# Moving three pieces of the SwiGLU "up" stage: an ACT split, a halved reciprocal and a divided last product

## The chip, the cores and the metric

One core of a Trainium2 chip runs the whole program. The metric is device time in microseconds (us) of one execution, from the host's request to the end on the core. TensorE is called PE (its weight loads PEld), VectorE DVE, ScalarE ACT, GpSimd POOL and SyncE, which issues the loads, SP.

## The reference

The program is one inference step of a two-layer decoder over 512 prompt tokens and 8 sample tokens. Every layer is a mixer with a residual and then a SwiGLU feed-forward block with a residual; layer 0 mixes with a gated convolution and a chunk MLP, layer 1 with a sparse attention. The change sits in the first half of the feed-forward block, which both layers have:

```python
D_MODEL = 1024
D_FF = ((8 * D_MODEL + 2) // 3 + 255) // 256 * 256   # 2816

def rmsnorm(x, g):
    xf = x.astype(jnp.float32)
    y = xf * lax.rsqrt(jnp.mean(xf * xf, axis=-1, keepdims=True) + EPS)
    return (y * g.astype(jnp.float32)).astype(x.dtype)

def swiglu(x, w_in, w_out):
    a, b = jnp.split(x @ w_in, 2, axis=-1)
    return (jax.nn.silu(a) * b) @ w_out

    # in each layer, for prompt xp and sample xs
    xp = xp + swiglu(rmsnorm(xp, norm_ffn[layer]), w_ffn_in[layer], w_ffn_out[layer])
```

## The kernel before, in words

Activations lie transposed, features on the 128 partitions and the 520 tokens (two halves of 260) along the free dimension. Every fp32 operand of a matmul is split into a high and a low part, and each product is three matmuls: high by high, high weight by low activation, low weight by high activation. For weights ACT writes the high part (`act_high`, line 706, 128x512) and POOL the low part (`pool_low`, line 714, raw minus high).

The stage that the change touches is the input projection of SwiGLU, called "up0" and "up1". Its 2816 columns a and 2816 columns b form 22 pairs of 128 columns (KF = 22). Each pair is computed as a block product with **seven** products instead of eight (Winograd's form): `A11`, `S1`, `S2`, `A12`, `S3`, `A22`, `S4`. S1 to S4 are sums and differences of weight blocks that DVE makes (`dve_sum`), from blocks that ACT first copies into PSUM (`act_copy`, line 694). A product is 4 quarters of 3 matmuls, so 12 matmuls of 128x260. PE's order for pair p is written out in `PE_SEQ`: A11(p), A22(p-1), S4(p-1), S1(p), S2(p), A12(p), S3(p), and then A11(p+1). The results are put together by:

- the copy of the first product, `first(p)` (line 965): ACT copies product A11 out of PSUM to `X1`. For p > 0 it waits for the last reader of the previous X1, the addition at line 909;
- `u2` (line 897), `u3` (lines 901 and 904), `up_rows` (909 adds X1 to A22's result, 911 multiplies by RSTD into TB) and `gate_rows` (916, 918) on DVE, then Silu on ACT (971), the gate (925), and the split of the result into G high (977) and G low (931), the operand of the next stage, "down".

PE waits for weights by a count on POOL's low parts (`u_lo`), and in some places for DVE: S3 waits for u2, A22 for u3, S2 also for the multiplication at 911, because it writes the PSUM bank that 911 reads. A12 waits for the X1 copy (`u_first`).

RSTD is the reciprocal root of the mean square per token. ACT writes the root (line 592), and DVE takes the reciprocal of all 520 columns at once in `norm_dve` (line 596) and clears ACC (597). The two lines are shared with other norms of the program; for the up stages they run at p = 1, between DVE's sum S2(1) and `up_rows(0)`.

The first pair's products are interleaved with the end of the stage before: `act_out_blocks` and `dve_out_blocks` finish the last tiles (m = 6, 7) of the output projection, turn its result into the right-hand blocks of the block product (lines 767 to 786 on ACT, 817 to 836 on DVE) and already split the first pair's weights. In the first pair PE computes three quarters of S2 and of A12, then the sum of squares (`pe_stat`), then their last quarters, because the last right-hand quarter comes late.

Each engine works through its own queue in program order; the order across engines is set by semaphores alone. SP loads the raw weights of pair p+2 when POOL has made the low part of A22(p).

The functions that the diff touches, with what calls them:

Of the kernel before, what the change touches and what calls it, by code (L numbers as in the profile page):

```python
# [21 lines left out]
HALF = T // 2  # L22
# [4 lines left out]
KF = FF // P  # L27
# [16 lines left out]
S0, U0 = {}, {}  # L44
# [128 lines left out]
def program(nc, a, out):  # L173
    ctx = ExitStack()
    with ctx:
# [351 lines left out]
        def plain(act):  # L527

            act.sem_inc(passed, 1)
# [213 lines left out]
            u_sum.on(ins)  # L743


        def act_out_blocks(act, l):

            name, i, gcol = f"out{l}", 2 * l + 1, G_FFN[l]
            for m in range(KD):
                q, x = m // 2, XT[:, m, :]  # L750
                gain = GAINS[:, gcol + m:gcol + m + 1]
                if m in (0, 2, 4):
                    split_next_wide(act, name, m // 4, m % 4 // 2)
                if m == 6:
                    act.wait_ge(tile_done.sem, U0[name] + 6)
                    act_copy(act, l, 0, "A21")
                    act_copy(act, l, 0, "A22")
                    act_high(act, l, 0, "A11")
                    act_high(act, l, 0, "S1")
                    act_high(act, l, 0, "S3")  # L760
                    act_copy(act, l, 0, "A12")
                    act_high(act, l, 0, "S2")
                if m == 7:
                    act_high(act, l, 0, "A12")
                act.wait_ge(tile_out.sem, m + U0[name] + 3)
                plain(act)
                b_full.on(act.activation(TA[:, m % 2, :], x, ACT.Copy, scale=gain))  # L767

                def square():
                    act.wait_ge(acc_ok.sem, m + 9 * (i - 1))  # L770
                    plain(act)
                    a_sq.on(act.activation(TG[:, m % 2, :], x, ACT.Square))
                if m % 2 == 0:
                    plain(act)
                    b_high.on(act.activation(x_part("B11", 0, q), x[:, 0:HALF], ACT.Copy, scale=gain))
                    act.wait_ge(b_turn.sem, 12 * l + 3 * q + 1)
                    plain(act)
                    b_high.on(act.activation(x_part("T1", 0, q), TB[:, 0:HALF], ACT.Copy))
                    square()
                else:  # L780
                    square()
                    plain(act)
                    b_high.on(act.activation(FB[:, 0:2, q, :], halves(x), ACT.Copy, scale=gain))
                    act.wait_ge(b_turn.sem, 12 * l + 3 * q + 3)
                    plain(act)
                    b_high.on(act.activation(HB[:, 1:4, q, :], HBR[:, 5:8, q, :], ACT.Copy))
# [53 lines left out]
        def pe_up(pe, l):  # L840

            name = f"up{l}"

            def product(p, op, qs=range(4)):
                par, other = (U0[name] + p) % 2, OTHER[op]
                bank = M[:, 2, 0:HALF] if op in ("S2", "S3", "A22") else PG[:, par, int(op in ("S1", "S4")), 0:HALF]
                wh, wl = home(WH, l, op), home(WL, l, op)
                for q in qs:
                    if p == 0:
                        pe.wait_ge(b_ok.sem, 16 * l + 4 * q + {"B11": 1, "T1": 2, "B21": 3, "B22": 3}.get(other, 4))  # L850
                    for n, w in ((0, wh), (1, wh), (0, wl)):
                        mm = pe.matmul(bank, w[:, q * P:(q + 1) * P], x_part(other, n, q),  # L852
                                       start=op in ("A11", "S1", "S2") and q == 0 and n == 0 and w is wh,
                                       stop=op in ("A12", "A22", "S4") and q == 3 and w is wl,
                                       skip_group_check=True)
                if q == 3:
                    (tile_done if op in ("A12", "S4") else u_prod).on(mm)

            for p, op in PE_SEQ:
                pe.wait_ge(u_lo.sem, 7 * KF * l + LO_NO[p, op])  # L860
                if op == "A11":
                    if p < 2:
                        pe.wait_ge(tile_out.sem, U0[name] + 1 + p)
                    elif p - 2 < LATE:
                        pe.wait_ge(g_ready.sem, G0[f"down{l}"] + p - 1)
                    else:
                        pe.wait_ge(t_gate.sem, KF * l + p - 1)
                if op == "S2" and p:
                    pe.wait_ge(tile_out.sem, U0[name] + 2 * p + 1)
                if op == "A12":  # L870
                    pe.wait_ge(u_first.sem, KF * l + p + 1)
                if op in ("S3", "A22", "S4"):
                    pe.wait_ge(u_add.sem, 4 * KF * l + 4 * p + {"S3": 1, "A22": 2, "S4": 3}[op])
                if (p, op) == (0, "S2"):
                    product(p, op, range(3))
                elif (p, op) == (0, "A12"):
                    product(p, op, range(3))
                    pe.wait_ge(u_sum.sem, 4 * KF * l + SUM_NO[0, "S4"])
                    pe_stat(pe, 2 * l + 1)
                    product(0, "S2", [3])  # L880
                    product(0, "A12", [3])
                else:
                    product(p, op)

        def dve_up(dve, l):
# [13 lines left out]
            def u3(p):  # L899
                wait_product(dve, l, p, "S3")  # L900
                u_add.on(dve.tensor_tensor(U3, turn(p)[1], X1[:, :], ALU.add))
                dve.wait_ge(u_add.sem, u_add.now)
                wait_product(dve, l, p, "S1")
                u_add.on(dve.tensor_tensor(W, turn(p)[2], U3, ALU.add))

            def up_rows(p):
                Y = turn(p)[1]
                wait_product(dve, l, p, "A22")
                u_add.on(dve.tensor_tensor(Y, Y, X1[:, :], ALU.add))
                dve.wait_ge(u_add.sem, u_add.now)  # L910
                tile_out.on(dve.tensor_tensor(halves(TB[:, :]), M[:, 2:4, 0:HALF], halves(RSTD[:, :]), ALU.mult))

# [20 lines left out]
            for p in range(KF + 1):  # L933
                if p:
                    u3(p - 1)
                    if p < KF:
                        dve_sum(dve, l, p, "S2")
                    if p == 1:
                        norm_dve(dve, 2 * l + 1)
                    up_rows(p - 1)  # L940
                    gate_rows(p - 1)
                    if p < KF:
                        dve_sum(dve, l, p, "S4")
                    gate(p - 1)
                if p < KF:
                    u2(p)
                if p + 1 < KF:
                    dve_sum(dve, l, p + 1, "S1")
                if 0 < p <= LATE:
                    g_low(p - 1)  # L950
                if p + 1 < KF:
                    dve_sum(dve, l, p + 1, "S3")
            for p in range(LATE, KF):
                g_low(p)

        def act_up(act, l):

            name, down = f"up{l}", f"down{l}"

            def first(p):  # L960
                wait_product(act, l, p, "A11")
                if p:
                    act.wait_ge(u_add.sem, 4 * KF * l + 4 * p)
                plain(act)
                u_first.on(act.activation(X1[:, :], PG[:, (U0[name] + p) % 2, 0, 0:HALF], ACT.Copy))

            def silu(p):
                both = sets((U0[name] + p) % 2)
# [10 lines left out]
            for p in range(KF):  # L979
                nxt = p + 1 < KF  # L980
                if p:
                    act_high(act, l, p, "S3")
                    act_copy(act, l, p, "A12")
                first(p)
                if p:
                    act_high(act, l, p, "S2")
                act_high(act, l, p, "A22")
                if nxt:
                    act_high(act, l, p + 1, "A11")
                if p == 0:  # L990
                    norm_act(act, 2 * l + 1)
                if p:
                    silu(p - 1)
                if p == 0:
                    act.wait_ge(a_std.sem, 2 * l + 2)
                if nxt:
                    act_copy(act, l, p + 1, "A21")
                    act_copy(act, l, p + 1, "A22")
                if 0 < p <= LATE:
                    g_high(p - 1)  # L1000
                act_high(act, l, p, "S4")
                if nxt:
                    act_high(act, l, p + 1, "S1")
                    act_high(act, l, p + 1, "A12")
# [1539 lines left out]
```

## Time and profile before

| | |
|---|---|
| median of 3 runs | 1343.24 us (1341.97 to 1344.81) |
| the profiled execution | 1342.97 us, its span 1341.2 us |
| mean granted TensorE clock | 0.995 of full |
| PE busy | 96% of the span |
| POOL, DVE, ACT busy | 60%, 54%, 48% |

The span runs from the first to the last instruction; the 1.77 us between it and the execution's time lie outside. PE's busy time is an upper figure: a matmul's duration overlaps the next one's, so that rows of 0.28 us start 0.12 us apart. The stages up0 and up1 lie at about 194 to 429 us and 966 to 1201 us; the stages down0 and down1 follow each.

### The profile page before, as it was taken

The page shows a single profiled execution, that of the slowest core. Times are in us where ns is not written, and L with a number is a line of the kernel's source. Part 1 is how long each engine was busy: PE and PEld are TensorE (multiplying, and loading weights), DVE is VectorE, ACT ScalarE, POOL GpSimd, SP SyncE. Part 2 cuts the span into 40 slices and gives each one's busy share as a digit, 9 for nine tenths or more (in the row PEclk, how much of TensorE's full clock was granted, in tenths as well). Part 3 has the DMA queues.
Part 4 walks back from the last instruction along what each step waited for, and adds up shares of the span by engine and source line. Part 5 has one row for each costly group of instructions (what it writes and reads, how often), then busy time and mean ns, then how long its engine had stood idle before and what let it go on. Part 6 is the DMA issues. An engine that isn't in the chain of part 4 may idle for free. (4 is left out here: it accounts for less than half of the span.)

```text
span 1341.2 us, 27440 instructions
## 1 busy us (share of the span) xinstructions
PE 1284.5 (96%) x10530; PEld 1193.9 (89%) x10530; DVE 721.1 (54%) x1213; ACT 644.7 (48%) x1160; POOL 808.9 (60%) x703
## 2 busy tenths in 40 slices
PE   6999999999999999999998998989999999999997
PEld 6999998999999999999986555657989999999997
DVE  5448587776776222211755767654877767761112
ACT  5412466666665233311313566653666666652332
POOL 7435447888888666644311554442578888886662
PEclk9999999999999999999999999999999999999999
DMA  5322223334333233337864042031233343333331
GB/s 182 95 95 69 91 64 95 95 110 112 95 95 97 87 86 88 115 96 167 195 143 89 18 139 66 1 87 32 64 95 96 105 116 96 95 97 87 87 102 68
DMA packets 211067, 127.87 MB, mean 95 GB/s; under 512 B 31868, under 2 KB 206004, under 8 KB 210958
## 3 DMA queue, kind: packets, MB, share of 16 engines
q1 hardware_dynamic: 210958, 126.40, 34.1%
q8 instruction: 70, 1.15, 0.4%
q14 instruction: 39, 0.32, 0.1%
HBM read 117.82 MB, written 5.38 MB: 92 GB/s over the span
## 5 line engine op out<-in xcount | busy, mean ns | idle before, releaser
L2177 POOL TENSOR_TENSOR WL<-WR,WH 128x512 fp32r<-128x512 f32 x236 | 317.6, 1377 | 274.6 <-ACT WH L537 274.6
L477 PE MATMUL PG<-G,WH 128*128 128x260 f32 x1856 | 298.9, 283 | 3.5 <-POOL WL L2177 3.5
L477 PEld LDWEIGHTS PG<-G,WH 128*128 128x128 f32 x1856 | 253.2, 188 | 6.3 <-POOL WL L2177 5.8
L537 ACT ACTIVATE WH<-WR 128x2048 fp32r<-128x2048 f32 x59 | 112.9, 1914 | 284.8 <-PE PG L477 249.2
L477 PE MATMUL PG<-H,WH 128*128 128x260 f32 x1312 | 216.6, 287 | 4.3 <-DVE H L2398 2.3
L852 PE MATMUL M<-HB,WH 128*128 128x260 f32 x1056 | 202.9, 290 | 8.4 <-POOL WL L714 4.9
L477 PE MATMUL PG<-G,WL 128*128 128x260 f32 x928 | 186.8, 282 | 0.0
L477 PEld LDWEIGHTS PG<-H,WH 128*128 128x128 f32 x1312 | 180.5, 190 | 6.4 <-POOL WL L2177 2.3
L714 POOL TENSOR_TENSOR WL<-WR,WH 128x512 fp32r<-128x512 f32 x132 | 169.5, 1297 | 21.1 <-ACT WH L706 21.1
L852 PEld LDWEIGHTS M<-HB,WH 128*128 128x128 f32 x1056 | 164.1, 190 | 18.1 <-POOL WL L714 15.6
L1323 POOL TENSOR_SCALAR PB<-PB,ST,GT 128x512 f32<-128x512 f32 (+3 forms) x128 | 80.1, 635 | 130.9 <-DVE ST L1776 130.4
L852 PE MATMUL PG<-FB,WH 128*128 128x260 f32 x528 | 149.3, 283 | 1.6 <-issue 1.6
L852 PE MATMUL M<-HB,WL 128*128 128x260 f32 x528 | 149.8, 284 | 0.0
L852 PE MATMUL PG<-FB,WL 128*128 128x260 f32 x528 | 148.8, 282 | 0.0
L477 PEld LDWEIGHTS PG<-G,WL 128*128 128x128 f32 x928 | 142.7, 188 | 0.0
L477 PE MATMUL PG<-H,WL 128*128 128x260 f32 x656 | 132.8, 284 | 0.0
L714 POOL TENSOR_TENSOR WL<-WLR,WH 128x512 fp32r<-128x512 f32 x90 | 114.6, 1294 | 3.3 <-ACT WH L706 3.3
L616 DVE TENSOR_TENSOR XT<-XT,PG 128x520 f32 x16 | 11.1, 697 | 174.7 <-PE PG L477 174.7
L477 PEld LDWEIGHTS PG<-H,WL 128*128 128x128 f32 x656 | 101.6, 189 | 0.0
L852 PEld LDWEIGHTS PG<-FB,WH 128*128 128x128 f32 x528 | 99.6, 189 | 1.9 <-issue 1.9
L852 PEld LDWEIGHTS M<-HB,WL 128*128 128x128 f32 x528 | 100.7, 191 | 0.0
L714 POOL TENSOR_TENSOR WL<-S2T,WH 128x512 fp32r<-128x512 f32 x44 | 57.5, 1306 | 71.5 <-ACT WH L706 71.5
(289 smaller groups left out, 2451.6 us busy)
## 6 DMA issues: line engine op xcount, KB each, us to landing
WR<-in_w_ffn_in SPq DMA_DIRECT2D x88, 512.0 KB, 4.9
WR<-in_w_in SPq DMA_DIRECT2D x32, 512.0 KB, 4.6
WR<-in_w_ffn_out SPq DMA_DIRECT2D x32, 384.0 KB, 4.1
WR<-in_w_ffn_out SPq DMA_DIRECT2D x32, 320.0 KB, 3.4
WR<-in_w_in SPq DMA_DIRECT2D x18, 256.0 KB, 4.4
WR<-in_w_out SPq DMA_DIRECT2D x8, 512.0 KB, 4.0
PST<-in_cache_kv SPq DMA_DIRECT2D x32, 128.0 KB, 2.3
WR<-in_w_out SPq DMA_DIRECT2D x16, 256.0 KB, 5.1
```

The costliest lines, as they stand in the source:

```text
L477: mm = pe.matmul(PG[:, par, hf, 0:HALF], w, x, start=(first and at_k == 0 and n == 0), stop=(last and at_k == nk - 1 and n == 2))
L537: w_hi.on(act.activation(WH[:, b, :], WR[:, b, :], ACT.Copy))
L616: tile_out.on(dve.tensor_tensor(row(XT, m), row(XT, m), sets((U0[name] + c) % 2), ALU.add))
L714: u_lo.on(pool.tensor_tensor(four(home(WL, l, op)), src, four(home(WH, l, op)).bitcast(F32), ALU.subtract))
L852: mm = pe.matmul(bank, w[:, q * P:(q + 1) * P], x_part(other, n, q), start=op in ("A11", "S1", "S2") and q == 0 and n == 0 and w is wh, st ...
L1323: p_ready.on(pool.tensor_scalar(pj, pj, ST8[:, 24 + o:25 + o], GT[:, i, g:g + 1], ALU.mult, ALU.mult))
L2177: low = pool.tensor_tensor(WL[:, b, c:c + 512], WR[:, b, c:c + 512], WH[:, b, c:c + 512].bitcast(F32), ALU.subtract)
```

## The change

- **ACT, p > 0**: the high part of S2(p) is split ahead of the X1 copy of the same pair instead of behind it. The order of the high parts among themselves stays.
- **ACT, p = 0**: the first X1 copy moves into `act_out_blocks`, at m = 7 behind the squares, ahead of the last splits of the right-hand blocks (783 and 786). It was the first instruction of `act_up`.
- **DVE**: the reciprocal of RSTD is taken in two halves of 260 columns. The first stands behind u2(0), ahead of the sum S1(1); the second stands inside `up_rows(0)`, between the addition at 909 and the multiplication at 911. The clearing of ACC goes to the end of p = 2. The sum S3(1) moves from the end of p = 0 to behind u3(0).
- **PE, last pair (p = 21)**: A12 is done in two parts, quarters 0 and 1 ahead of S3 and quarters 2 and 3 behind it.

```diff
+        def act_first(act, l, p):
+
+            wait_product(act, l, p, "A11")
+            if p:
+                act.wait_ge(u_add.sem, 4 * KF * l + 4 * p)
+            plain(act)
+            u_first.on(act.activation(X1[:, :], PG[:, (U0[f"up{l}"] + p) % 2, 0, 0:HALF], ACT.Copy))
+
         def act_out_blocks(act, l):
...
                     square()
+                    if m == 7:
+                        act_first(act, l, 0)
                     plain(act)
                     b_high.on(act.activation(FB[:, 0:2, q, :], halves(x), ACT.Copy, scale=gain))
...
+                elif (p, op) == (KF - 1, "A12"):
+                    product(p, op, range(2))
+                elif (p, op) == (KF - 1, "S3"):
+                    product(p, op)
+                    product(p, "A12", range(2, 4))
                 else:
                     product(p, op)
...
+            def rstd(hf):
+
+                dve.wait_ge(a_std.sem, 2 * l + 2)
+                r = RSTD[:, hf * HALF:(hf + 1) * HALF]
+                (rstd_ok if hf else vec).on(dve.reciprocal(r, r))
+                if hf:
+                    dve.wait_ge(vec.sem, vec.now)
+                    dve.wait_ge(rstd_ok.sem, rstd_ok.now)
+
             def up_rows(p):
                 Y = turn(p)[1]
                 wait_product(dve, l, p, "A22")
                 u_add.on(dve.tensor_tensor(Y, Y, X1[:, :], ALU.add))
+                if p == 0:
+                    rstd(1)
                 dve.wait_ge(u_add.sem, u_add.now)
                 tile_out.on(dve.tensor_tensor(halves(TB[:, :]), M[:, 2:4, 0:HALF], halves(RSTD[:, :]), ALU.mult))
...
             for p in range(KF + 1):
                 if p:
                     u3(p - 1)
+                    if p == 1:
+                        dve_sum(dve, l, p, "S3")
                     if p < KF:
                         dve_sum(dve, l, p, "S2")
-                    if p == 1:
-                        norm_dve(dve, 2 * l + 1)
                     up_rows(p - 1)
                     gate_rows(p - 1)
                     if p < KF:
...
                 if p < KF:
                     u2(p)
+                if p == 0:
+                    rstd(0)
                 if p + 1 < KF:
                     dve_sum(dve, l, p + 1, "S1")
                 if 0 < p <= LATE:
                     g_low(p - 1)
-                if p + 1 < KF:
+                if p and p + 1 < KF:
                     dve_sum(dve, l, p + 1, "S3")
+                if p == 2:
+                    acc_ok.on(dve.memset(ACC[:, :], 0.0))
...
                 if p:
                     act_high(act, l, p, "S3")
                     act_copy(act, l, p, "A12")
-                first(p)
-                if p:
                     act_high(act, l, p, "S2")
+                    act_first(act, l, p)
                 act_high(act, l, p, "A22")
```

## Rows read from the trace of the kernel before

**Rows 1.** The page's busy line: time, share of the span, instructions.

```profile
PE 1284.5 (96%) x10530; PEld 1193.9 (89%) x10530; DVE 721.1 (54%) x1213; ACT 644.7 (48%) x1160; POOL 808.9 (60%) x703
```

**Rows 2.** The chain that ended last, up1 and down1: start, us, what.

```profile
1056.20 8.79 POOL WL L714 x7
1064.99 1.53 issue
...
1209.30 119.01 PE PG L477 x990
```

**Rows 3.** Who waited for whom: total us, times, longest.

```profile
PEld M L852 <- POOL WL L714: 15.6, 42, 2.7
...
PE M L852 <- POOL WL L714: 4.9, 2, 2.5
```

**Rows 4.** Timeline of one pair of up1, all engines: start, us, instruction, idle before.

```profile
1057.55 0.30 PEld L852 LDWEIGHTS M<-HB,WH 128*128 128x128 f32 x2 [0.26 <-POOL WL L714]
1057.56 0.51 PE L852 MATMUL M<-HB,WH 128*128 128x260 f32 x2
...
1059.10 0.28 PE L852 MATMUL PG<-FB,WH 128*128 128x260 f32 x1
...
1059.30 0.43 DVE L897 TENSOR_TENSOR TA<-M,X 128x260 f32<-128x260 f32 x1 [0.56 <-PE M L852]
...
1062.17 0.43 DVE L901 TENSOR_TENSOR TA<-M,X 128x260 f32<-128x260 f32 x1 [0.64 <-PE M L852]
...
1062.98 0.68 DVE L737 TENSOR_TENSOR S2T<-M,WHR 128x512 f32<-128x512 f32 x1
...
1063.70 1.30 POOL L714 TENSOR_TENSOR WL<-WR,WH 128x512 fp32r<-128x512 f32 x1
...
1065.03 0.44 DVE L909 TENSOR_TENSOR M<-M,X 128x260 f32<-128x260 f32 x1 [1.37 <-PE M L852]
...
1065.50 0.70 DVE L911 TENSOR_TENSOR TB<-M,RSTD 128x520 f32<-128x520 f32 x1
...
1065.58 0.39 ACT L965 ACTIVATE X<-PG 128x260 f32<-128x260 f32 x1 [2.21 <-DVE M L909]
...
1065.86 0.63 ACT L706 ACTIVATE WH<-S2T 128x512 fp32r<-128x512 f32 x1
...
1066.57 1.30 POOL L714 TENSOR_TENSOR WL<-S2T,WH 128x512 fp32r<-128x512 f32 x1 [1.57 <-ACT WH L706]
...
1067.59 0.28 PE L852 MATMUL PG<-HB,WL 128*128 128x260 f32 x1
...
1067.92 0.39 PE L852 MATMUL M<-HB,WH 128*128 128x260 f32 x1
```

**Rows 5.** Timelines of ACT, DVE and PE, the first pairs of up1.

```profile
968.58 0.71 ACT L783 ACTIVATE FB<-XT,GAINS 128x520 fp32r<-128x520 f32 x1
...
970.16 0.37 ACT L965 ACTIVATE X<-PG 128x260 f32<-128x260 f32 x1
...
971.59 1.28 ACT L592 ACT_TABLE_LOAD   x1
972.88 0.69 ACT L592 ACTIVATE RSTD<-M,BASE 128x520 f32<-128x520 f32 x1
...
976.87 0.58 ACT L694 ACTIVATE M<-WR 128x512 f32<-128x512 f32 x1
...
974.36 0.69 DVE L727 TENSOR_TENSOR WLR<-M,WR 128x512 f32<-128x512 f32 x1 [0.70 <-ACT M L694]
...
976.96 3.39 DVE L596 RECIPROCAL RSTD<-RSTD 128x520 f32<-128x520 f32 x1
...
970.63 0.36 PE L852 MATMUL PG<-FB,WH 128*128 128x260 f32 x1 [0.72 <-issue]
...
983.64 0.80 PE L852 MATMUL M<-HB,WH 128*128 128x260 f32 x2 [2.46 <-POOL WL L714]
```

**Rows 6.** One stretch behind that break: busy us (count) per engine, PEclk, DMA.

```profile
983.60:986.70 3.10, 3.06 (x14) 3.06 (x15) 0.80 (x3) 3.09 (x6) 3.10 (x3) 0.51 0.02 5
```

**Rows 7.** PE's timeline, last pair of up1.

```profile
1197.50 0.48 PE L852 MATMUL M<-HB,WH 128*128 128x260 f32 x2 [0.61 <-DVE TA L901]
```

More of the change, by code:

```diff
@@ L958, in act_up @@
             name, down = f"up{l}", f"down{l}"
-            def first(p):
-                wait_product(act, l, p, "A11")
-                if p:
-                    act.wait_ge(u_add.sem, 4 * KF * l + 4 * p)
-                plain(act)
-                u_first.on(act.activation(X1[:, :], PG[:, (U0[name] + p) % 2, 0, 0:HALF], ACT.Copy))
             def silu(p):
@@ L983, in act_up @@
                     act_copy(act, l, p, "A12")
-                first(p)
-                if p:
                     act_high(act, l, p, "S2")
+                    act_first(act, l, p)
                 act_high(act, l, p, "A22")
```

## The prediction

> **What bounds the kernel now.** I read the busy line first: PE is busy for 96% of the span and no other engine for more than 60% [rows 1]. So a gain has to come out of PE's own gaps, or out of stretches at a lower clock. Next the chain of waits: in up1 it does not run along PE. It repeats, 19 times, seven low parts of POOL (8.79 us) and 1.53 us in which POOL stands, and only in down1 does it run along PE, 990 matmuls in 119.01 us, 0.120 us each [rows 2]. The view of who waited says how much PE pays: its weight loads waited for POOL 42 times, 15.6 us in all, and two matmuls for 4.9 us more [rows 3]. 42 is 21 pairs in each of two layers, so one wait per pair behind the first.
>
> The timeline of one pair shows which wait it is [rows 4]. PE starts S2 at 1057.56 and the next pair's S2 at 1067.92, a period of 10.36 us. From the first matmul of A12 (1059.10) to the last of S1 (1067.59) there are 72 matmuls, 71 steps in 8.49 us, 0.1196 each, with no gap. All 84 matmuls at that step are 10.05 us, so **0.31 us per pair** is lost, all of it at S2: the weight load starts when POOL has the low part (1066.57 + 1.30 = 1067.87). POOL's low part waits 1.57 us for ACT's high part (1065.86); that stands in ACT's queue behind the X1 copy (1065.58), which had ACT idle for 2.21 us until DVE's addition at 909 (1065.03 to 1065.47). The sum itself, S2T, was ready at 1063.66. This closes a loop: A22, addition, X1 copy, high part, low part, S2, and so on to the next A22.
>
> **The change part by part.**
>
> *S2's high part ahead of the X1 copy.* It can start when S2T is ready and ends near 1064.35 (0.63 us). POOL is then still in the low part that began at 1063.70 and takes S2 at about 1065.0, done at 1066.3, against the 1067.59 + 0.12 = 1067.71 at which PE would reach S2: 1.4 us early [rows 4]. The other condition of S2, the multiplication at 911, ends at 1066.20. The copy itself does not move, as its addition ends at 1065.47, after the high part is out of the way; what follows it on ACT (high parts of A22 and A11) comes 0.6 us earlier, and the load that SP issues behind A22's low part comes earlier too. What is late next: S3 starts at 1059.10 + 12 x 0.12 = 1060.54 and needs u2, which ends at 1059.73; A22 starts 24 steps after S3, at 1063.4, and needs u3 at 1062.60. Both have 0.7 us or more to spare [rows 4]. POOL's seven low parts are 8.79 us of 10.05 [rows 2]. So PE becomes the bound with no gap: 0.31 us in 20 pairs of each layer, **12.4 us**. Bounds: by down1's 0.1202 per matmul the period would be 10.10, and the sum 10.5; nothing if another wait of equal size appears.
>
> *The start.* Before, PE waits 2.46 us for the first S2 of pair 1, until 983.64 [rows 5], in both layers (4.9 us, two times [rows 3]). Here the row behind it is the 3.39 us reciprocal at 976.96, which holds back the addition at 909 and with it copy, high part and low part. Afterwards DVE does, from the end of the root at 973.57: half a reciprocal, S1(1), u3 with its second addition, S3(1), then it waits for ACT (high part of S3, copy of A12), S2(1), the addition, the other half, the multiplication. Half a reciprocal is 1.70 if its time goes by columns, 3.39 if it did not shrink at all; sums of 512 and of 260 columns take 0.68 and 0.43, so something per instruction is fixed, and I take 1.74. In steps: 973.6 + 1.74 + 0.6 (S1; back to back these start 0.6 apart) = 976.0; u3 0.45 and 0.35 = 976.8; S3 0.68 = 977.5; ACT 0.55 + 0.58 [rows 5] = 978.7; S2 0.6 = 979.3; addition 0.4 = 979.7; half 1.74 = 981.4; multiplication 0.70 = **982.15**. The low part of S2(1) is done earlier: 979.4 + 0.63 + 1.30 = 981.3. So S2(1) starts at about 982.15 instead of 983.64: 1.5 us per layer, **3.0**. Bounds: at no shrinking 985.5, a loss of 1.8 per layer; with 1.70 each 982.05.
>
> The first half is not hidden: it delays S1(1) and u3(0), so that PE can't begin A22(0) before 976.0 + 0.43, about 976.5. The early X1 copy lets PE go on at 969.75 (970.63 less 0.72 idle, and 0.16 by which a lone matmul's 0.28 outlasts its step) instead of 970.63 [rows 5], 0.9 us, but PE gives that back at A22(0) and at S2(1), since the root does not come earlier: it starts when ACT's table load ends (972.87), and ACT has the same instructions up to there. Worth nothing by itself. Behind the early copy on ACT stand the two splits of the last right-hand quarter, 783 and 786; they wait with it for A11(0). PE did S1(0) and nine matmuls of S2(0) up to 969.75, 21 steps, so A11(0) ended near 967.3, before ACT gets there at 968.58 [rows 5]. Clearing ACC moves to pair 2, into DVE's wait for S3 (0.64 us idle there [rows 4]; it takes 0.49 and the next stage asks for ACC much later): nothing.
>
> *The clock behind the break.* After the 2.46 us wait PE runs at 0.51 of its clock, the lower level (1.2 GHz), for 3.1 us: 14 matmuls where 26 would fit [rows 6], so 12 x 0.12 = 1.4 us lost. A22(0), S4(0) and S1(1) are 36 steps, from 976.5 to 980.8, so the new break before S2(1) is 980.8 to 982.15, about 1.35 us. The 1.0 us break that ends at 970.63 [rows 5] is followed by matmuls 0.12 apart. 1.35 is nearer to 1.0 than to 2.7, so I take full clock: 1.4 us in each layer, **2.8**. Bounds: nothing, or this.
>
> *The table load on ACT* lies twice in this stretch, ahead of the root and ahead of the first Silu. The row shows 1.28 us, and the root starts 0.01 us behind it [rows 5]. The Trainium skill ("ScalarE: Activation LUTs", section "What ACT_TABLE_LOAD costs") puts a switch at about 2.66 us, 1.28 of load and 1.38 of drain. The trace shows the first and not the second. By the page the first Silu, and with it S3(1), would come an estimated 0.65 us later in each layer, and the sum would be 18.4 instead of 19.7.
>
> *The last pair.* A22(21) waits 0.61 us for u3 [rows 7]; with the pipeline refilling (0.48 against 0.40 for two matmuls, and the 0.16 by which a lone matmul's end outlasts its step) that is 0.85 us. Six matmuls of A12 now stand there: 6 x 0.12 = 0.72. S3 in turn follows S2 after only six matmuls, and u2 ends at 1059.73 where PE would be at 1059.10 + 0.72 = 1059.82 [rows 4]: it just fits. So 0.75 per layer, **1.5**; bounds 0.6 and 0.85.
>
> **The sum**: 12.4 + 3.0 + 2.8 + 1.5 = 19.7 us. The stages behind shift along, since their first waits hang on the end of S4(21). The profiled execution took 1342.97 us, 0.27 below the median: **1323.3 us**.
>
> **The rivals.**
> 1. *The start gives little*: the clock still falls after the 1.35 us break, or a half reciprocal costs more than half. Without the clock's 2.8 it is 1326.1; with full-price halves as well (loss of 3.6 instead of a gain of 3.0) 1332.7. For it: the breaks of pair 0 and 1 lie closer together than before. Against: the reciprocal is one of four of equal length, and its 6.5 ns per column is far above the sums' 1.3, so columns dominate.
> 2. *A new wait in the steady pairs takes part of the 0.31*: the nearest are u2 before S3 and u3 before A22, 0.7 us ahead. If half is taken, 1329.5; if all is, 1335.7.
> 3. *The first Silu's table load costs more than its row*: Silu's input (918) comes near 983.2, and the load ends near 982.7, so 1.4 us more would make Silu, gate, u2(1) and S3(1) some 0.65 us later in each layer: 1324.6. Against it is the row [rows 5]. It is the case that the Trainium skill's figure, above, would make.
> 4. *The other side: ACT's queue.* The high part of S2 now stands ahead of the X1 copy, so a late S2T holds X1, and A12 with it. The new loop runs S3, high part of S3, copy of A12, S2T, high part of S2, X1 copy, A12, S3. It decides from the point at which it exceeds the old 10.36 us. From 1062.0 (S3 done) X1 would be there near 1064.8, and A12 asks for it at 1069.4: 4.6 us in hand. Were S2T 5 us late, each of 40 pairs would take 0.4 us more than before, 16 us, less 7.3 from start and end: 1352. S2T ends 2 us before even the old X1 copy began [rows 4], so this is remote.
> 5. *The weights were not what S2 waited for*, the multiplication at 911 being the real bound: then only start and end move, 1335.7. It ended 1.7 us before S2 began [rows 4].
>
> **How the numbers follow.** The forecast (1320 to 1325) has 0.66; rival 1 0.14; rival 2 0.10; rival 3 0.02; rival 5 0.03; rival 4 0.03; something stronger than the forecast 0.02. The runs of before spread by 1.4 us to either side, and 0.2% (2.7 us) is about what a measurement of this kernel can tell from no change. The range 1319.5 to 1331 takes in the forecast with this scatter, rival 1 without the full-price case and half of rival 2. Only the last two rivals, and rival 2 with more than its whole price, end near or above 1340.6: faster 0.93, same 0.04, slower 0.03.
>
> **What would show it.** Right: POOL's low part of S2T without its 1.57 us wait and ending over a microsecond before PE needs it, no wait of PE's weight loads for line 714 in the steady pairs, S2 every 10.05 us; two reciprocals of 260 columns, 1.7 us each, in each layer; S2(1) some 1.5 us earlier against the start of the stage, released by the multiplication at 911, with a full clock behind it; A22(21) behind S3 without an idle row over 0.15 us. Wrong: pairs of more than 10.15 us, or a PE wait on DVE in each of them; a reciprocal half over 2 us; a clock below 1 in the first pairs.

## The result and the profile after

The changed kernel took 1330.14 us (median of 4 runs, 1323.76 to 1333.35) against 1342.92 (1341.97 to 1344.81) for the kernel before: a ratio of 0.9897 (95% interval 0.9859 to 0.9936), so 12.8 us faster where 19.7 was forecast. The sign and the range held; the point 1323.3 missed by 6.8 us. The profiled execution took 1330.37 us, its span 1328.6.

The page's busy line of the changed kernel, which answers to [rows 1]:

```profile
PE 1279.2 (96%) x10530; PEld 1193.6 (90%) x10530; DVE 721.0 (54%) x1215; ACT 648.7 (49%) x1160; POOL 812.9 (61%) x703
```

It says little: the shares hardly move. The chain that ended last, in the stretch of up1 where [rows 2] showed POOL (start, us, what), and the view of who waited (engine, line, releaser, total us, times, longest), which answers to [rows 3]:

```profile
1047.04 2.88 PE PG L862 x24
...
1054.22 1.44 PE PG L862 x12
1057.09 2.88 PE PG L862 x24
```

```profile
PEld M L862 <- POOL WL L714: 3.2, 4, 1.2
...
PE M L862 <- DVE TA L912: 2.1, 2, 1.0
```

The chain now runs along PE through the steady pairs, and it repeats every 1057.09 - 1047.04 = 10.05 us instead of 10.36. The 42 waits of PE's weight loads for POOL have become 4, two at the start of each up stage, and a new pair of waits for DVE's line 912 (u2), 1.0 us each, has come. The timeline of one pair of up1 in the changed kernel, which answers to [rows 4]:

```profile
1045.02 0.68 DVE L737 TENSOR_TENSOR S2T<-M,WHR 128x512 f32<-128x512 f32 x1
...
1045.83 0.63 ACT L706 ACTIVATE WH<-S2T 128x512 fp32r<-128x512 f32 x1 [0.43 <-DVE S2T L737]
...
1046.54 1.29 POOL L714 TENSOR_TENSOR WL<-S2T,WH 128x512 fp32r<-128x512 f32 x1 [0.16 <-ACT WH L706]
...
1047.62 0.39 ACT L752 ACTIVATE X<-PG 128x260 f32<-128x260 f32 x1 [1.16 <-DVE M L933]
...
1049.76 0.40 PE L862 MATMUL M<-HB,WH 128*128 128x260 f32 x2
```

ACT splits S2T 0.13 us after the sum, and the X1 copy (line 752 now) stands behind it. POOL's wait for the high part is 0.16 us instead of 1.57, its low part ends at 1047.83, and PE begins S2 at 1049.76 without an idle row, 1.9 us later.

Where the 12.6 us of the span came from is read by stages. In the windows (stretch, its length, then busy us and count of PE, PEld, DVE, ACT, POOL, PEclk, DMA share, GB/s) of the kernel before, an up stage runs from its first matmul to the first of the next stage; the middle row is the attention stage between the two. Then the same windows of the changed kernel:

```profile
193.84:429.00 235.16, 230.09 (x1854) 224.84 (x1853) 162.16 (x289) 154.08 (x282) 192.42 (x153) 0.99 0.35 97
706.13:930.32 224.19, 200.63 (x1721) 130.43 (x1719) 137.81 (x300) 116.20 (x343) 92.24 (x140) 0.99 0.23 59
965.79:1200.62 234.83, 229.88 (x1854) 224.62 (x1853) 162.04 (x288) 154.04 (x282) 192.28 (x153) 0.99 0.35 97
```

```profile
193.30:418.58 225.28, 223.50 (x1854) 222.17 (x1853) 162.08 (x290) 155.86 (x282) 193.85 (x153) 1.00 0.36 101
696.22:927.47 231.25, 208.43 (x1720) 135.06 (x1719) 137.71 (x300) 116.33 (x343) 92.75 (x140) 0.96 0.21 57
962.95:1188.06 225.11, 223.44 (x1855) 222.28 (x1853) 161.92 (x289) 156.08 (x282) 193.82 (x153) 1.00 0.36 101
```

The up stages gave 9.88 and 9.72 us, 19.6 together. All that lies outside these three stages differs by 0.1 us. Attention, of which the change touches nothing, took 7.06 us more, at a mean granted clock of 0.96 instead of 0.99. PE ran at half clock there in two stretches. The first begins 2 us behind the end of an idle break of 1.42 us that both kernels have (the changed kernel's is shown under copy_late). The break and the windows behind it, of before:

```profile
718.04 0.63 PE L1430 MATMUL M<-CKT,P 64*128 64x32 f32 x8 [1.42 <-DVE TC L1727]
...
718.00:721.00 3.00, 2.96 (x42) 2.64 (x42) 2.72 (x4) 0.21 (x1) 2.83 (x3) 1.00 0.53 121
721.00:730.00 9.00, 9.00 (x96) 6.95 (x96) 4.12 (x8) 3.64 (x12) 1.14 (x2) 1.00 0.00 0
```

The windows behind it in the changed kernel:

```profile
708.00:711.00 3.00, 2.97 (x36) 2.56 (x36) 2.71 (x4) 0.22 (x1) 2.85 (x3) 0.87 0.47 108
711.00:720.00 9.00, 9.00 (x60) 7.27 (x60) 1.29 (x2) 0.84 (x1) 1.14 (x2) 0.50 0.00 0
```

Both second windows are 9 us of full PE, with 96 matmuls in the one and 60 in the other. The other stretch comes some 20 us later. There the clock of the kernel before fell too, but for 3.4 us instead of 10.2. Windows inside it, of before and then of the changed kernel:

```profile
734.20:737.50 3.30, 3.30 (x12) 2.04 (x14) 1.81 (x3) 0.59 (x1) 1.04 (x3) 0.50 0.00 0
```

```profile
730.80:740.90 10.10, 9.35 (x38) 4.30 (x36) 2.36 (x8) 3.13 (x10) 2.00 (x4) 0.50 0.00 0
```

Together PE stood at half clock for 20.5 us of the changed kernel's attention stage, and for 3.4 us of before's. Whether the change causes this or only met it is what several of the experiments ask.

### The profile page after: what moved, and what is told of

The parts are those of the page before. It is cut to its first block and busy times, and to the rows that moved or that the text cites. A ratio compares the mean times of both kernels' runs of the same rounds, so it can differ in the third digit from the quotient of the medians.

```text
span 1328.6 us, 27442 instructions
## 1 busy us (share of the span) xinstructions
PE 1279.2 (96%) x10530; PEld 1193.6 (90%) x10530; DVE 721.0 (54%) x1215; ACT 648.7 (49%) x1160; POOL 812.9 (61%) x703
## 5 line engine op out<-in xcount | busy, mean ns | idle before, releaser
L477 PE MATMUL PG<-G,WH 128*128 128x260 f32 x1856 | 298.8, 283 | 4.0 <-POOL WL L2199 4.0
L862 PE MATMUL M<-HB,WH 128*128 128x260 f32 x1056 | 196.4, 284 | 3.5 <-DVE TA L912 2.1
L862 PEld LDWEIGHTS PG<-FB,WL 128*128 128x128 f32 x528 | 99.5, 188 | 0.0
L862 PE MATMUL PG<-G,WH 128*128 128x260 f32 x352 | 99.4, 282 | 0.0
```

The lines of the kernel that those rows point to most:

```text
L477: mm = pe.matmul(PG[:, par, hf, 0:HALF], w, x, start=(first and at_k == 0 and n == 0), stop=(last and at_k == nk - 1 and n == 2))
```

## The experiments

The stages of each kernel in its own profiled execution, in us, cut as above; in brackets, how long PE's granted clock was at half in the attention stage:

| kernel | up0 | attention (of it at half clock) | up1 | span |
|---|---|---|---|---|
| before | 235.16 | 224.19 (3.4) | 234.83 | 1341.2 |
| changed | 225.28 | 231.25 (20.5) | 225.11 | 1328.6 |
| s2_only | 227.12 | 225.76 (6.8) | 226.94 | 1326.7 |
| no_s2 | 231.83 | 227.54 (10.2) | 231.42 | 1338.4 |
| silu_early | 224.08 | 228.58 (13.7) | 223.88 | 1324.1 |
| hold | 225.31 | 226.76 (10.2) | 225.18 | 1323.8 |
| after_again | 225.30 | 231.07 (20.5) | 225.18 | 1328.1 |
| before_again | 233.66 | 225.69 (6.8) | 233.54 | 1339.2 |
| silu_hold | 224.01 | 224.08 (3.4) | 223.92 | 1317.5 |
| copy_late | 225.76 | 224.80 (6.8) | 225.62 | 1322.4 |
| after_third | 225.28 | 230.79 (20.5) | 225.14 | 1328.6 |
| after_fourth | 225.29 | 230.76 (17.1) | 225.17 | 1328.1 |
| before_hold | 235.21 | 222.63 (0) | 233.52 | 1337.6 |
| whole | 226.03 | 225.21 (6.8) | 225.90 | 1324.1 |

The up stages repeat within 0.1 us between executions of the changed kernel; attention is what scatters. So parts of the change are priced by the up stages, not by the total. The bracket accounts for attention in all fourteen rows, whichever kernel it is: a straight line, 222.6 us and 0.42 us for each us at half clock, meets every one of them within 0.9 us.

**s2_only**: on the kernel before, only the order of S2's high part and the X1 copy.

```diff
-                first(p)
                 if p:
                     act_high(act, l, p, "S3")
                     act_copy(act, l, p, "A12")
                     act_high(act, l, p, "S2")
+                first(p)
```

> The kernel before with one part of the change alone: for p > 0 the high part of S2 stands ahead of the X1 copy. If S2's low part was what PE waited for, each up stage goes from 234.9 and 234.6 us to about 228.5 (20 waits of 0.31 us, 6.3 us), with no wait of the weight loads for line 714 in the steady pairs, and the 2.46 us break of pair 1 hardly moves. If the multiplication at 911 or PE's own step is the bound, the up stages stay above 234. The attention stage between the two is not touched: 224 us if its clock stays as in the kernel before, up to 231 if the loss seen after the change is one of the clock.

1328.51 us (1328.08 to 1331.1, 4 runs), ratio 0.9869 (0.9833 to 0.9906). Its up stages gain 8.04 and 7.89, of which 20 steady pairs are 6.2; the other 1.7 to 1.8 lie at the start. There PE's wait before S2(1), which was expected hardly to move, fell from 2.46 us to 0.93, and the clock stayed full behind it; a new wait of 1.04 us for u2 ahead of S3(1) took part of that back. PE's timeline at S2(1):

```profile
975.40 0.48 PE L852 MATMUL M<-HB,WH 128*128 128x260 f32 x2 [0.93 <-DVE TB L911]
```

Pair 1 has the new order too, and its S2 had stood behind the copy that the reciprocal delayed. So the one-line move alone carries four fifths of what the up stages gain, the break at the start included (against before_again, whose up stages had full clock, 6.5 and 6.6 of 8.4).

**no_s2**: on the changed kernel, the old order of these two for p > 0, all else as changed.

```diff
+                    act_first(act, l, p)
                     act_high(act, l, p, "S2")
-                    act_first(act, l, p)
```

> The changed kernel with that part undone: the high part of S2 stands behind the X1 copy again. By the forecast's sum the up stages take 225.0 and 224.8 plus 6.3, so 231.2 each: start and end of the stage keep their 3.5 us per layer. If the parts are not additive (the start only pays because the steady pairs wait no more) they come near 234.

1340.15 us (1334.83 to 1344.5, 10 runs), ratio 0.995 (0.9928 to 0.9973). Up stages of 231.83 and 231.42: start and end alone give 3.33 and 3.41, and S2 on top of them 6.55 and 6.31, the steady pairs' 6.2. On its own S2 gave 8.0, so that 8.0 and 3.4 add up to 1.5 more than the 9.8 of both together. Nearly all of it is the fall of the clock behind the break in [rows 6], which neither run has and which is so counted twice: against before_again, where the clock did not fall either, the parts give 6.5 and 1.8 in up0 and 6.6 and 2.1 in up1, and both together 8.4 in each.

**silu_early**: on the changed kernel, one column through Silu ahead of the first real one.

```diff
+                if p == 1:
+                    act.activation(BASE[:, 2 * P + 4:2 * P + 5], BASE[:, 2 * P + 5:2 * P + 6], ACT.Silu)
                 if p:
                     silu(p - 1)
```

> The changed kernel with a one-column Silu on ACT ahead of the wait of the first Silu, so that ACT's table load runs while ACT would stand idle. If that load, which starts only when the Silu's input is there, makes u2(1) late and with it S3(1), PE's 1.2 us break before S3(1) goes and each up stage is 1.2 us shorter: about 223.7. If DVE's own queue holds u2(1) (the gate stands ahead of it), the break stays over 0.8 us.

1327.72 us (1325.92 to 1328.96, 4 runs), ratio 0.9861 (0.9825 to 0.9897). ACT's timeline of up1:

```profile
974.12 1.28 ACT L1015 ACT_TABLE_LOAD   x1
975.41 0.20 ACT L1015 ACTIVATE BASE<-BASE 128x1 f32<-128x1 f32 x1
975.83 0.59 ACT L994 ACTIVATE PG<-PG 128x520 f32<-128x520 f32 x1 [0.22 <-DVE PG L944]
```

The table is loaded while ACT waits anyway, the real Silu starts 0.22 us after ACT got there, PE no longer waits ahead of S3(1), and the up stages are 1.20 and 1.23 us shorter. That is the price of the load's place in the changed kernel.

**hold**: on the changed kernel, matmuls on constant data into a place that nobody reads, in the 1.42 us break and in a later wait of attention.

```diff
+            def fill(n):
+                for _ in range(n):
+                    pe.matmul(M[0:64, 3, 384:512], IDENT[:, 0:64], BASE[:, 0:P], start=False, stop=False, skip_group_check=True)
...
                 if x == 16:
+                    fill(6)
                     pe.wait_ge(cs_out.sem, 1)
...
+                        if hu == 0 and q == q_step[0] + 3:
+                            pe.wait_ge(csh_ok.sem, 2)
+                            fill(12)
                         turn(hu, q, kt)
```

> The changed kernel with fill-in matmuls (64 columns of weights, 128 columns, into PSUM columns that nobody reads) on PE in two breaks of the attention stage, 6 ahead of the wait for the compressed scores (1.7 us) and 12 in the first turn (3.1 us). If the 7.1 us that attention takes longer after the change are the granted clock's, it stays at 1.00 there and the stage takes 224 us or less, the whole about 1321 to 1324, and the runs lie within 3 us of each other. If the stage is longer because of a new wait, it takes 231 us at full clock too.

1323.65 us (1321.16 to 1325.58, 4 runs), ratio 0.9822 (0.9785 to 0.9859). The clock is full behind the 1.42 us break. This profile alone does not show that filling did it, as s2_only, silu_early, copy_late and whole leave the break empty and have full clock behind it too. Attention took 226.76, not the 224 or less that was expected, and the runs spread by 4.4 us instead of 3, since the clock still falls at other places (from 729, 770 and 893 us, for 3.4 us each). Hold's windows at the filled break and at the first of these falls:

```profile
705.00:708.00 3.00, 3.00 (x34) 2.60 (x34) 1.96 (x5) 0.00 (x0) 0.49 (x1) 1.00 1.13 206
725.00:735.00 10.00, 8.41 (x57) 4.56 (x54) 3.80 (x11) 4.12 (x13) 2.81 (x5) 0.83 0.00 0
```

**after_again** and **before_again**: the two kernels themselves, once more with profiles. 

> The changed kernel once more, beside the kernel before on the same chip, for the scatter of both. If the clock in the attention stage falls in both kernels alike and at random, the two medians lie 17 to 21 us apart (the 19.6 us of the up stages), single runs of both spread by about 10 us, and in both the longer runs have the lower mean clock. If the change itself lengthens the attention stage, the medians lie 11 to 14 us apart and the stage is near 231 us in this profile too.

1330.05 us (1321.99 to 1333.49, 6 runs), ratio 0.9888 (0.9861 to 0.9915), and attention at 231.07: both are what was expected if the change itself lengthens the stage.

> The kernel before once more, for a second profile. Its runs in the last call went from 1341 to 1351 us at mean clocks of 0.993 to 0.985. If that is the attention stage's clock, the profile of a run that is longer than 1343 us has up stages of 234.9 and 234.6 us as before and the surplus over 224.2 us in the attention stage, in stretches at half clock. If the surplus lies in the up stages, the 19.6 us are themselves a matter of the run.

1341.84 us (1340.33 to 1349.35, 8 runs), ratio 0.9997 (0.9978 to 1.0016). Its attention is longer by 1.5, its up stages shorter by 1.50 and 1.29 than in [rows 6]'s execution. PE's timeline at S2(1), and a window as long as that of [rows 6] behind it:

```profile
982.95 0.51 PE L852 MATMUL M<-HB,WH 128*128 128x260 f32 x2 [2.48 <-POOL WL L714]
```

```profile
982.90:986.00 3.10, 3.05 (x25) 3.05 (x26) 1.52 (x4) 3.09 (x6) 3.10 (x3) 1.00 0.00 0
```

Practically the same break, 2.48 us for 2.46, and 25 matmuls at full clock behind it where [rows 6] has 14 at half. So this fall of the clock is not a property of the kernel: it comes in one execution and not in the next. (before_hold has it in up0 and not in up1: 235.21 and 233.52.)

**silu_hold**: silu_early and hold together.

> The changed kernel with both additions: the early Silu on ACT and the fill-in matmuls in two breaks of the attention stage. If they are independent, the up stages take 223.8 and 223.6 us as with the early Silu alone, and the total lies 2.4 us under that of the fill-in alone: 1319 to 1323 us, some 25 us under the kernel before. If the earlier arrival only moves the attention stage onto other falls of the clock, the total is no better than with the fill-in alone, 1321 to 1326.

1319.81 us (1318.3 to 1320.68, 5 runs), ratio 0.982 (0.9802 to 0.9837) against 1343.36 for the kernel before: the best version, and the one with the least scatter (2.4 us, where after_again's six runs spread by 11.5 on the same chip). Its attention:

```profile
694.01:918.09 224.08, 204.86 (x1756) 134.08 (x1754) 137.75 (x300) 116.21 (x343) 92.24 (x140) 0.99 0.23 59
```

**copy_late**: on the changed kernel, the first X1 copy back at the head of `act_up`.

```diff
-                    if m == 7:
-                        act_first(act, l, 0)
...
                     act_first(act, l, p)
+                else:
+                    act_first(act, l, 0)
```

> The changed kernel with the first X1 copy back at the start of the up stage's ACT work. The forecast called its move worth nothing: up stages of 225.0 and 224.8 us as with the change, within 0.1. If the 0.9 us by which it lets PE go on count, they are 225.9 and 225.7.

1324.18 us (one run). The up stages are 0.48 and 0.51 longer, between the two expectations: the early copy is worth 0.5 per layer, not nothing. This execution had the same idle break as the changed kernel. PE's timeline of the changed kernel, then of copy_late, and copy_late's windows behind it:

```profile
708.03 0.64 PE L1452 MATMUL M<-CKT,P 64*128 64x32 f32 x8 [1.42 <-DVE TC L1749]
```

```profile
707.72 0.64 PE L1452 MATMUL M<-CKT,P 64*128 64x32 f32 x8 [1.42 <-DVE TC L1749]
```

```profile
708.00:711.00 3.00, 3.00 (x44) 2.60 (x44) 2.40 (x2) 0.53 (x1) 3.00 (x3) 1.00 0.41 96
711.00:720.00 9.00, 9.00 (x96) 6.82 (x94) 4.40 (x11) 3.62 (x12) 0.83 (x2) 1.00 0.00 0
```

Same break, same work, full clock: attention took 224.80, with 6.8 us at half clock further on.

**after_third** and **after_fourth**: the changed kernel again, to see whether its attention is always the long one.

> The changed kernel a third time, for the scatter alone. So far 8 of its 10 runs lie in the upper half of their 12 us (1327 to 1333), of the kernel before about half of 42. If that is chance, these runs and those of the kernel before fill their ranges alike, and the medians of all runs lie 16 to 20 us apart. If the change puts the attention stage where the clock falls more often, at least three quarters of the runs are above 1327 again and the medians stay 13 to 14 us apart.

1326.26 us (1322.32 to 1332.27, 6 runs), ratio 0.9869 (0.9841 to 0.9898). The medians lie 17.4 us apart, where 12.8 and 13.3 were seen, and three of the six runs are above 1327, as expected of chance; the profile's attention is again the long one, 230.79.

> The changed kernel a fourth time, for the scatter. So far 11 of its 16 runs lie more than 5.4 us above its fastest (1322.0), of the kernel before 24 of 59 above its own (1340.0). If the fall of the clock in the attention stage is chance in both, the share of the changed kernel comes down towards a half; if the change makes it more frequent, it stays at two thirds or more.

1327.93 us (1323.64 to 1329.85, 6 runs), ratio 0.987 (0.9845 to 0.9895); attention 230.76. Of all 22 runs of the changed kernel 14 lie more than 5.4 us above its fastest, of 70 of the kernel before 28 lie so above theirs. The 0.64 of the changed kernel lies between the half that was expected of chance and the two thirds of the other case. In both kernels these longer runs are those at the lower clock: their mean granted clock is 0.989, and that of the shorter ones 0.993. All four profiles of the changed kernel have the fall behind the 1.42 us break, and so has no_s2; the profiles of before, before_again, s2_only, silu_early, copy_late and whole, where the break is unfilled as well, do not. The four profiled executions of the changed kernel are also alike (1329.85 to 1330.37) where its other 18 runs go from 1321.99 to 1333.49. So they show that the fall repeats in the executions whose profile was kept, and not how often it comes in the others.

**before_hold**: hold's edit on the kernel before.

> The kernel before with the fill-in matmuls in the same two breaks of the attention stage and nothing else. If the clock's fall there is no matter of the change, it helps this kernel as it did the changed one: runs within 5 us of each other and a median of 1338 to 1341, 19 to 20 us above the changed kernel with the same fill-in (1323.7). If the clock falls there only after the change, nothing is gained: 1343.

1339.43 us (1339.15 to 1342.02, 12 runs) against 1343.61, ratio 0.997 (0.9957 to 0.9983). Filling helps the kernel before too, by 4.2 us, and twelve runs lie within 2.9 us where 17 of the kernel before on the same chip scatter over 10 (1340.0 to 1350.07). The profile has no half clock in attention at all. So falls of the clock in attention are there without the change. The median lies 15.8 us above hold's, where 19 to 20 was expected, because hold's attention still took 4.1 more.

**whole**: on the changed kernel, the reciprocal in one piece, where the kernel before had it.

```diff
                         dve_sum(dve, l, p, "S2")
+                    if p == 1:
+                        dve.wait_ge(a_std.sem, 2 * l + 2)
+                        rstd_ok.on(dve.reciprocal(RSTD[:, :], RSTD[:, :]))
+                        dve.wait_ge(rstd_ok.sem, rstd_ok.now)
                     up_rows(p - 1)
...
-                if p == 0:
-                    rstd(0)
...
-                if p == 0:
-                    rstd(1)
```

> The changed kernel with one reciprocal of 520 columns, between S2(1) and the addition at 909, in place of the two halves; all else of the change stays. By its rows the chain of pair 1 is: sums 0.9 us earlier without the first half, then 3.39 instead of 1.77, so the multiplication at 911 and all behind it 0.7 us later and each up stage 225.5 to 226.0 instead of 225.0. If the halves carry the 1.5 us per layer that the forecast gave them, it is 226.5.

1325.92 us (one run). The up stages are 0.75 and 0.79 longer: that is what the halves are worth, as the rows said, and half of the 1.5 that the forecast gave them.

## Why the prediction was right, and where it failed

*S2's high part: right, in mechanism and size.* A period of 10.05 us per pair was forecast and measured, PE is the chain, and no new wait took its place (rival 2), nor did ACT's queue (rival 4). Rival 5 is out, since undoing this one move (no_s2) costs 6.4 us per layer, where 6.2 was forecast for it.

*The start: right in sum (2.9 per layer forecast, clock included), wrong in its path, twice, and by luck the two errors cancel.* What is left of the up stages' 9.88 and 9.72 after 6.2 for the steady pairs and 0.74 for the end (below) is 2.94 and 2.78. The timelines of DVE, ACT and PE over the first pairs of up1, changed kernel, answer to [rows 5]:

```profile
970.53 1.78 DVE L925 RECIPROCAL RSTD<-RSTD 128x260 f32<-128x260 f32 x1 [0.68 <-ACT RSTD L592]
...
973.56 0.68 DVE L731 TENSOR_TENSOR WHR<-WR,M 128x512 f32<-128x512 f32 x1
974.33 0.69 DVE L737 TENSOR_TENSOR S2T<-M,WHR 128x512 f32<-128x512 f32 x1
...
975.35 1.77 DVE L925 RECIPROCAL RSTD<-RSTD 128x260 f32<-128x260 f32 x1
...
977.21 0.70 DVE L937 TENSOR_TENSOR TB<-M,RSTD 128x520 f32<-128x520 f32 x1
978.28 0.71 DVE L944 TENSOR_TENSOR PG<-PG,RSTD 128x520 f32<-128x520 f32 x1
...
974.91 0.58 ACT L694 ACTIVATE M<-WR 128x512 f32<-128x512 f32 x1
...
979.09 1.28 ACT L994 ACT_TABLE_LOAD   x1 [1.73 <-DVE PG L944]
...
978.05 0.47 PE L862 MATMUL M<-HB,WH 128*128 128x260 f32 x2 [0.20 <-DVE TB L937]
...
982.19 0.48 PE L862 MATMUL M<-HB,WH 128*128 128x260 f32 x2 [1.04 <-DVE TA L912]
```

First, the step "then it waits for ACT (high part of S3, copy of A12), S2(1)" is wrong. The sum S2 counts two earlier copies, those of A21 and A22, and S3; the copy of A12 (974.91) came after it. S2(1)'s sum stands right behind S3(1) at 974.33, and PE began S2(1) at 978.05, after 0.20 us instead of the forecast 1.35. The stage starts 2.84 us earlier than before (962.95, 965.79), so in before's time this is 980.89, 1.26 earlier than the forecast 982.15. What released it is the multiplication, as forecast (line 937 now), and the clock stayed full up to it and behind it, so rival 1 did not come.

Second, the table load. Rival 3 and the forecast both had Silu's load run ahead, ending near 982.7, before Silu's input. It stands behind the wait for that input: ACT had stood idle for 1.73 us, and the load starts at 979.09, 0.10 us after line 944 ended (978.28 + 0.71). So it delays Silu, the gate, u2(1) and so S3(1), for which PE waits 1.04 us. silu_early takes it back, 1.20 and 1.23 per layer. Its price is the row's 1.28 us and no more: in silu_early the next instruction starts 0.01 us behind it, as in [rows 5]. The Trainium skill ("ScalarE: Activation LUTs", section "Step-by-step: what each stage is for") says that the compiler places the load right before the ACTIVATE that needs it. The trace agrees; the forecast had read its length and not its place.

*The halves* took 1.78 and 1.77 us where 1.74 was forecast. *The early copy*, priced at nothing "since the root does not come earlier", is worth 0.5 per layer, and the root does come earlier: its table load starts 5.55 us after the stage's first matmul (968.50 less 962.95), and 5.80 us in before (971.59 less 965.79) and in copy_late. The other 0.2 is DVE's: in copy_late its addition for pair 0 waits 0.21 us for PE, which is later there, and in the changed kernel it does not wait.

*The clock's 2.8 us* hold against the one profile of before on which [rows 6] stand. In before_again the clock behind the same break stayed full, and its up stages stand 8.38 and 8.43 above the changed kernel's: 16.8 in such a pair of runs, and 19.6 where the clock fell. The forecast took a coin's side for a constant. The Trainium skill ("TensorE: Matmul & The Clock Gate", section "What's actually happening") says that the count of slow matmuls at the start of one and the same kernel differs from run to run. The two executions here show such a difference in the middle of a kernel: 14 matmuls at half clock and 25 at full in 3.1 us behind the same break.

*The last pair: right.* PE's timeline of the changed kernel, which answers to [rows 7]:

```profile
1182.49 0.28 PE L862 MATMUL PG<-FB,WL 128*128 128x260 f32 x1
1182.66 0.47 PE L862 MATMUL M<-HB,WH 128*128 128x260 f32 x2
...
1184.76 0.28 PE L862 MATMUL PG<-FB,WL 128*128 128x260 f32 x1
1184.94 0.48 PE L862 MATMUL M<-HB,WH 128*128 128x260 f32 x2
```

No idle row: the steps at both ends of A12's second half are 0.17 and 0.18 instead of 0.12, so 0.85 less 0.11 is 0.74 per layer, where 0.75 was forecast.

*The step that failed: "The stages behind shift along".* They did, except attention, which took 7.06 us more in the execution of the record and within 0.6 us of that in all four profiles of the changed kernel. The forecast of 19.7 less 7.06 is 12.6, which is the span's. Nothing in that stage was changed. PE stood there at half clock for 20.5 us instead of 3.4; by the line through the fourteen profiles (0.42 us for each) these 17.1 us cost 7.2, about the whole difference.

The total stayed in the range by luck: its upper part had been opened for rivals 1 and 2, which did not come, and no term or rival held a loss in attention. The scatter that the range allowed for was that of three runs, 1.4 us to either side; 70 runs of the kernel before go from 1340.0 to 1351.2.

What is shown: the loss is clock, the kernel before has falls of the clock in the same stage, and filling the breaks gains from it without the change (before_hold). What stays open: why the fall behind the 1.42 us break is in all four profiles of the changed kernel, and so whether the change makes it more likely. That the stage starts some 10 us earlier (696.22 instead of 706.13) does not explain it alone, since copy_late's starts at 696.00 and silu_early's at 695.58 without the fall, and no_s2's at 703.29 with it. Over all runs the changed kernel (22, mean 1328.2) lies 16.3 us below the kernel before (70, mean 1344.5), 95% interval 14.8 to 17.9; without the 13 runs of before on a chip on which the changed kernel itself did not run it is 15.8, and fastest against fastest 18.0 (1321.99, 1340.0).

## What to carry to other kernels

Where one engine serves two chains in turn, look which of its queue's instructions is ready first: swapping two lines of ACT gave four fifths of the gain, because the ready one stood behind one that hung on PE through another engine. Price a moved stall against more than one execution: a break that costs clock in one run may not in the next, and a stage that the change doesn't touch can take back a third of the gain. A table load can be pulled out of a chain by one dummy column of the same function, and a wait of PE that costs clock can be filled with matmuls that nobody reads; both together gave 10 us on top of the change (1319.81 against 1330.05).

## What the runs showed of the hardware

- After one and the same idle break of 1.42 us among small matmuls the granted clock was 0.50 in one kernel's execution (60 matmuls in 9 us) and 1.00 in another's (96 in 9 us); after 2.46 and 2.48 us it was 0.51 in one execution of the kernel before and 1.00 in another. The lower level is 1.2 GHz, the higher 2.4.
- In fourteen profiles of ten kernels the length of the attention stage goes by the time that PE stood at half clock in it: 222.63 us with none, 231.25 with 20.5 us, 0.42 us for each us.
- Eighteen added matmul calls in two breaks (36 more matmuls in the trace: 1756 in silu_hold for 1720) narrowed the runs of the kernel before from 10 us (17 runs) to 2.9 (12 runs) on one chip. With them silu_hold's five runs lie within 2.4, where after_again's six spread by 11.5 on the same chip; but silu_early's four, with the breaks unfilled, lie within 3.0 too.
- In the changed kernel the table load waited for what its own instruction waits for: it starts at 979.09, 0.10 us behind the end of line 944, after 1.73 us in which ACT stood idle. In silu_early, where its instruction waits for nothing, it starts at 974.12, right behind the instruction before it (972.96 + 1.14).
- A reciprocal on DVE of 260 columns takes 1.77 us against 3.39 for 520: by these two 0.15 us are fixed and 6.2 ns come for each column.
